# Early counting of places, an earlier gather, and the embedding product inside a first group of experts written apart

## The reference

```
x1 = LN1(alpha*x + W_out [pool_group(x) | mlstm_group(x)])
x2 = LN2(alpha*x1 + MoE(x1))            # top 4 of 32 experts, softmax router
y  = x2 + sigmoid(x2 @ W_pg) * (p @ W_ple)

logits = x1 @ w_router + b_router;  top_v, top_e = top_k(logits, 4);  gates = softmax(top_v)
for each expert e, for the tokens that chose it:
    h = xb @ w1[e] + b1[e]                                  # 1024 x 2048
    glu = min(h[:, ::2], 7);  lin = clip(h[:, 1::2], -7, 7)
    out = (glu * sigmoid(1.702*glu) * (lin + 1)) @ w2[e] + b2[e]   # 1024 x 1024
    MoE[token] += gate * out
```

## Time and profile before

| | us |
|---|---|
| three runs | 1112.04, 1112.07, 1110.48 |
| median | 1112.04 |
| span of the profiled execution | 1109.9 |
| TensorE busy | 1076.3 (97%) |
| VectorE busy | 436.3 (39%) |

### The profile page before, as it was taken

The page is one execution under the profiler, slowest core; times in us unless marked ns, Lnnn a source line. Parts: engine busy times, 40 slices in busy tenths (PEclk is TensorE's granted clock), DMA queues, the critical chain, the costliest instruction groups (busy, mean ns, idle before and its releaser), DMA issues.

```text
span 1109.9 us, 15169 instructions
## 1 busy us (share of the span) xinstructions
PE 1076.3 (97%) x5600; PEld 430.6 (39%) x5600; DVE 436.3 (39%) x1109; ACT 159.2 (14%) x306; POOL 82.2 (7%) x107
## 2 busy tenths in 40 slices
PE   8999999999999999999999999999999999999998
PEld 6787433333333333333333333333333333333334
DVE  1637773333333333333333333333333333323245
ACT  1532241000000000000000000000000000000033
POOL 0856511000000000000000000000000000000000
PEclk9999999999999999999999999999999999999999
DMA  9988989999999999999999999999999999999961
GB/s 315 267 340 332 311 343 390 428 427 428 429 428 430 428 428 430 427 429 429 427 429 429 426 430 429 428 429 429 428 427 429 427 426 429 427 425 429 428 271 40
DMA packets 52608, 440.63 MB, mean 397 GB/s; under 512 B 10544, under 2 KB 17964, under 8 KB 27381
## 3 DMA queue, kind: packets, MB, share of 16 engines
q1 hardware_dynamic: 52057, 439.53, 95.8%
q0 software_dynamic: 368, 0.57, 0.2%
q10 hardware_dynamic: 148, 0.07, 0.0%
HBM read 436.61 MB, written 3.77 MB: 397 GB/s over the span
## 4 chain that ended last, share of the span: by engine, by line
PE 64%; DMA 23%; DVE 9%; issue 2%; ACT 1%; POOL 1%; DVEq 0%; SPq 0%; POOLq 0%; ACTq 0%
PE bank L990 25%; DMA ring<-in_w_mlp 22%; PE bank L1061 16%; PE bank L590 6%; PE bank L949 4%; DVE proj L1619 3%; PE bank L769 3%; PE bank L1141 3%; DVE proj L1616 2%; DVE proj L1614 2%; PE bank L1042 1%; PE bank L962 1%; PE bank L984 1%; PE bank L1050 1%; DMA ring<-in_w_in 1%
## 5 line engine op out<-in xcount | busy, mean ns | idle before, releaser
L990 PE MATMUL bank<-ring,proj 128*64 128x512 f32 x2024 | 460.9, 597 | 13.1 <-DMA ring<-in_w_mlp 12.6
L1580 DVE SCALAR_TENSOR_TENSOR xT<-bank,proj,xT 128x512 f32<-128x512 f32 x128 | 90.2, 746 | 423.8 <-PE bank L949 422.5
L990 PEld LDWEIGHTS bank<-ring,proj 128*64 128x64 f32 x2024 | 140.8, 136 | 288.9 <-issue 260.5
L1061 PE MATMUL bank<-ring,pool_side 128*64 128x512 f32 x1024 | 226.8, 595 | 0.4 <-ACT pool_side L1951 0.4
L1061 PEld LDWEIGHTS bank<-ring,pool_side 128*64 128x64 f32 x1024 | 71.3, 137 | 133.5 <-issue 129.7
L1945 ACT ACTIVATE proj<-proj 128x256 f32<-128x256 f32 x64 | 26.7, 417 | 545.2 <-DVE proj L1613 544.2
L590 PE MATMUL bank<-xT,ring 128*128 128x264 f32 x320 | 77.1, 400 | 1.5 <-DMA ring<-in_w_in 1.5
L1571 DVE TENSOR_SCALAR proj<-bank,ln_rows_of_pairs 128x64 f32<-128x64 f32 x256 | 67.4, 335 | 24.5 <-PE bank L962 24.5
L949 PE MATMUL bank<-mixT 64*128 64x512 f32 x264 | 74.5, 641 | 0.9 <-ACT mixT L1954 0.5
L590 PEld LDWEIGHTS bank<-xT,ring 128*128 128x128 f32 x320 | 62.3, 197 | 14.3 <-issue 3.2
L928 PE MATMUL bank<-xreg,proj 128*64 128x512 f32 x248 | 58.7, 592 | 0.0
(11 more groups left out here) (369 smaller groups left out, 632.2 us busy)
## 6 DMA issues: line engine op xcount, KB each, us to landing
ring<-in_w_mlp SPq DMA_DIRECT2D x190, 2048.0 KB, 28.9
ring<-in_w_in SPq DMA_DIRECT2D x10, 1024.0 KB, 13.0
ring<-in_w_out SPq DMA_DIRECT2D x4, 1024.0 KB, 8.3
ring<-in_w_ple_gate SPq DMA_DIRECT2D x4, 1024.0 KB, 28.1
xreg<-in_x_prompt SPq DMA_DIRECT2D x4, 512.0 KB, 4.6
ring<-q_row SPq DMA_DIRECT2D x1, 2048.0 KB, 6.9
ring<-k_row SPq DMA_DIRECT2D x1, 2048.0 KB, 6.9
out<-ring SPq DMA_DIRECT2D x1, 2048.0 KB, 14.8
```

What stands on the lines that cost most here:

```text
L990: last = pe.matmul(bank[q][BLOCK * t:BLOCK * (t + 1), :], xgT[:, k % 4, k // 4, :], rows_[:, col:col + 512], start=False, stop=(k == KD - 1))
L1061: last = pe.matmul(bank[4][BLOCK * h:BLOCK * (h + 1), :], aT[:, m, BLOCK * t:BLOCK * (t + 1)], w[:, k % 2, 512 * h:512 * h + 512], start=F ...
L1580: ins = STT(total[:, c, s], ins_bank[h][:, :], gate_table[:, c, bass.ds(n, 1)], total[:, c, s], ALU.mult, ALU.add)
```

## The change

TensorE: the four early counts now stand ahead of `turn_quarter`, the sums of the early chunks between `turn_quarter` and `router(1, 6)`, and no embedding product stands in the handover. The first four experts are written apart from the loop, which starts at expert 4. In expert 0 a part of `early_embedding` follows each of the units 1 to 4, and `early_samples` follows the combination behind unit 5. The embedding of chunk 1 goes to banks 2 and 3 instead of 4 and 7, and before the gather for expert 1 TensorE waits until ScalarE has copied all three products. ScalarE's copies of the products move behind casts that it does for the sample rows. VectorE no longer waits for the products. SP loads `late[1]` behind pair n = 22 and no longer ahead of pair n = 16. `early_pT` moves to a space of its own, since `gates` is dead by then.

```
@@ banks @@
-        EMBED_BANKS = {0: (bank[1], bank[6]), 1: (bank[4], bank[7]), 2: (bank[5],)}
+        EMBED_BANKS = {0: (bank[1], bank[6]), 1: (bank[2], bank[3]), 2: (bank[5],)}
@@ SP @@
             load_next(14)
-            sp.wait_ge(sem("ple_ps"), 3)
-            load_late(1)
             for n in range(SLOTS, UNITS * STEP, 2):
                 sp.wait_ge(sem("units_used"), n - SLOTS + 2)
                 load_next(n)
+                if n == SLOTS + 6:
+                    sp.wait_ge(sem("ple_ps"), 3)
+                    load_late(1)
@@ TensorE, handover @@
-            turn_quarter(0)
-            turn_quarter(1)
-            router(1, 6)
...
                       start=False, stop=True).then_inc(sem("pos_ps"), 1)
+            turn_quarter(0)
+            turn_quarter(1)
             pe.matmul(bank[3][:, 0:3 * EXPERTS], ones16[0:1, :], far_row, start=True, stop=False)
             count_places(0, (1,))
             count_places(2, (1,))
+            router(1, 6)
             logit_rows(2)
-            pe.wait_ge(sem("ple_in"), 16)
-            early_samples()
...
             count_places(1, ()).then_inc(sem("pos_ps"), 1)
-            early_embedding(0, (0,))
@@ TensorE, expert(n, j, closing=0, opening=False) @@
+                    if opening and 1 <= k <= 4:
+                        early_embedding((k - 1) // 2, ((k - 1) % 2,))
...
                         combine(2, (j + 1) % 2)
+                        if opening:
+                            pe.wait_ge(sem("hotT_done"), 1)
+                            early_samples()
+
+                if opening:
+                    pe.wait_ge(sem("ple_done"), 3)
@@ TensorE, start of the experts @@
-            early_embedding(0, (1,))
-            early_embedding(1, (0, 1))
             pe.wait_ge(sem("places_split"), 1)
-            pe.wait_ge(sem("ple_done"), 1)
...
-            with pe.Fori(0, npass * EXPERTS - 2 * STEP, STEP) as n:
+            pe.wait_ge(sem("ple_in"), 16)
+            for j in range(STEP):
+                expert(j, j, opening=(j == 0))
+            with pe.Fori(STEP, npass * EXPERTS - 2 * STEP, STEP) as n:
@@ VectorE @@
-            dve.wait_ge(sem("ple_ps"), 3)
@@ ScalarE @@
-            act.wait_ge(sem("ple_ps"), 1)
-            act.copy(embedded_samples, EMBED_BANKS[2][0][:, 0:256]).then_inc(sem("ple_done"), 1)
...
-            embedded_early(0)
+            act.nop().then_inc(sem("out_done"), 1)
...
-            act.wait_ge(sem("ple_ps"), 3)
             act.copy(part_high, xtok[0:SAMPLES, 2, :]).then_inc(sem("part_cast"), 1)
+            embedded_early(0)
...
             act.copy(sample_parts[32:32 + SAMPLES, :], part_mid).then_inc(sem("sample_moved"), 1)
+            embedded_early(1)
...
             act.copy(sample_parts[0:SAMPLES, :], part_high).then_inc(sem("sample_moved"), 1)
+            act.wait_ge(sem("ple_ps"), 3)
+            act.copy(embedded_samples, EMBED_BANKS[2][0][:, 0:256]).then_inc(sem("ple_done"), 1)
```

12 lines of the change are left out of this document (5 added, 7 removed).

## The result

| | median, us | lowest to highest | executions |
|---|---|---|---|
| before | 1110.48 | 1108.33 to 1112.07 | 7 |
| changed | 1115.68 | 1112.07 to 1118.95 | 7 |

The ratio is 1.0043, with an interval from 1.0028 to 1.0058: the change makes the kernel 4.8 us slower by the ratio, 5.2 by the medians. The forecast was 2.0 us slower, 1114.0. The time lies in the range and the direction is the forecast one, but the size forecast was less than half of what came. That the time lies in the range is in part luck: the forecast built on 1112.04, the median of three runs, where seven have 1110.48, and this makes up for 1.6 us of the effect that it missed.

What follows compares the result with a forecast made beforehand. DMA engines bound the kernel: the fifth pair's limit moves from 181.7 to 183.2, +1.6 us, or +2.4 with small packets; taken as +2.0 on 1112.04, giving 1114.0 us. Own range 1113.2 to 1115.2; 8 in 10, 1110.4 to 1116.2.

Steps and rivals of the forecast that it cites:

- What bounds the kernel: Whole run: DMA engines set the end, at 428 GB/s, from the moment they are never idle again; TensorE's work doesn't.
- the tail doesn't change: End of the run: what follows the remaining bytes at 428 GB/s takes as long as before.
- The handover starts expert 0 earlier by 2.8 us: Handover ahead of expert 0: without the embedding products, its biases start at 150.85 against 153.64.
- the register load: Behind `spread_places`: loading the number of passes loses its cover and delays the biases by 0.8 us, bounds 0 and 1.3.
- `late[1]` in the full stream: Between fourth and fifth pair: the load, free before in an empty queue, now takes 2.45 us of DMA time.
- The sum of +2.0: Whole kernel: +1.6 us by the model, +2.4 with small packets of other queues, taken as +2.0.
- the later releases: Expert 0: its added products make the third, fourth and fifth pair releases 0.8, 1.8 and 1.6 us later.
- The rival with the slow clock: Handover: one 3.5 us stretch at the 1.2 GHz level costs 1.75 us, giving 1115.8; chance 0.12.
- No change: Rival, handover and expert 0: TensorE catches up partly, `late[1]` takes only dry time; +0.5 us, 1112.5; chance 0.17.
- the first release carries: Rival, first pair release: the queue resumes 2.8 us earlier and never runs dry afterwards, giving 1109.2; chance 0.13.
- No early start: Rival, handover: expert 0 starts less than 1 us earlier, the five products are paid in full, 1116; chance 0.03.

Runs made afterwards that it cites:

- the kernel that starved the queue for a moment in expert 7: Changed kernel with embedding products in expert 7, eight experts written apart, `late[1]` loaded behind the load group of experts 4 to 7: 1124.65 us, ratio 1.0137.
- load ahead: Changed kernel with TensorE's load of the number of passes moved ahead of the turning of the gathered rows: 1114.31 us, ratio 1.0032.
- the fillers: Four added products with unused results (256, 256, 384 and 512 columns) in the handover's waits of the changed kernel: 1112.75 us, ratio 1.0015.
- the thin products: Kernel before with its early embedding products 16 columns wide instead of 512 and 256, all in their old places: 1111.78 us, ratio 1.0007.

## Why the prediction was right in direction and wrong in size

**What bounds the kernel.** Right in the main. TensorE's waits for weights and its pace hardly move, and among kernels with the same loop the end follows the bytes left at 200: 2.4 MB more, 5.6 us. Between the two kinds of loop 0.6 to 2 us more come up behind 200, against the words that the tail doesn't change; and in the kernel that starved the queue for a moment in expert 7 a busy TensorE helped nothing.

**The handover starts expert 0 earlier by 2.8 us.** Right to 0.1 us (153.64 - 3.4 - 147.55 = 2.7), with its parts: the 0.8 us of the register load, and in expert 0 1.06 us for each embedding part where 1.0 was taken. The releases came 0.1 to 0.6 us after those of the sum, and expert 0's second product was 2.2 us late and not 1.6.

**`late[1]` in the full stream, 2.45 us.** Right in kind and somewhat too large: the load alone moved costs 2.0 us, the load taken out of the changed kernel gives back 0.5 to 1.9, most likely 1.4. It is the largest single part of the loss at an equal clock. Products and load don't simply add: with half of the products back in the waits the kernel is only 1.2 and 0.6 us above the kernel before (at 1.000 and 0.998), though this load is where the change put it.

**The sum of +2.0.** At an equal clock the change costs 2.6 to 2.7 us, within the forecast's own range of +1.2 to +3.2. What remains of the difference, 0.6 us, fits the later releases, and it also fits what comes up behind 200 in every kernel with the experts written apart (the last pair is under way 0.9 us longer); no run separates the two.

**The rival with the slow clock.** This is the step that was mis-sized, and what makes the measured loss more than twice the forecast one. It was named, but with a chance of 0.12, one stretch of 3.5 us and a price of 1.75 us. It was argued away with the stretch from 140.0 to 143.5, where TensorE was busy 2.43 of 3.50 us and the clock stayed full. But that stretch is followed, in the kernel before, by the samples, the gather and an embedding part, one behind the other from 144.30 to 149.5 without a gap; in the changed kernel the gather is followed by waits of 0.71, 0.21 and 0.80. The argument looked at the emptiest stretch by itself and not at what came behind it, which is just what the change takes away. And the fall doesn't last one stretch: in the long profiles the clock stays low for 13.7 us, until the products stand close again in expert 0, at a price of 4.8 us at the first release. It adds 1.7 us to the mean. The runs show that the products are the cause by taking them away from the kernel before (11 of 11 below 0.998, against 8 of 35 beside it) and by putting other products into the changed one (0 of 11, against 10 of 16). Half of them put back (6 of 12) doesn't settle anything. Taken together, the kernels without these products and without others in their place have 30 of 40 executions below 0.998 (changed 10 of 16, without the load 6 of 7, the two with the products in expert 7 3 of 4 and 5 of 5, load ahead 6 of 8), those with all of them in the handover 12 of 107. The moved load (1 of 11) and the moved counts (1 of 22) don't bring it. How the products act is less clear: a fall can begin at 141.0, ahead of the place where they stood, and the fillers, one of which runs at 140.3, filled waits on both sides of it. What is shown is that without dense products the clock stays low longer.

**No change, and the first release carries.** Both fell. The queue ran dry after the second and third release (172 and 166 GB/s), and the fifth was the limit. "No early start" fell with the biases at 147.55.

What stays open: why the fall comes in some executions of one program and not in others, and whether the embedding products keep it from starting or only from lasting; what of it the thin products' median hides; and what the experts written apart cost by themselves. No version here is clearly faster than the kernel before; the one with only the counts moved is its equal.

## What to carry to other kernels

Products that look as if they delay a chain of small dependent steps may be what keeps TensorE's clock from staying low through it: before moving them out, count which waits they fill, and put something in their place. Where a full DMA queue bounds the kernel, a load is free only in the gap in which the queue is empty, and every load that waits on SP holds up all loads behind it. And when two executions of a program differ, sort them by their mean granted clock before comparing medians; here this separates 2.65 us of the change from 1.7 us of the clock, and without it one experiment would have been read the wrong way round.

## What the runs showed of the hardware

The granted clock fell to the 1.2 GHz level in a handover in which TensorE never waited longer than about 0.8 us at once, and stayed there for 13.7 us with the engine busy 3.10, 2.69 and 2.76 of 3.40 us (already at the slower pace), and then, from 151.1 to 154.7, 3.60 of 3.60; from 154.7 on it was full again. The Trainium skill, TensorE: Matmul & The Clock Gate, section "A second HAM failure mode: psum-queue depth-cycling", says that frequent small pauses between groups of products, and not only long idle stretches, can make the clock swing. This case's traces agree in so far as the only waits in the handover are of 0.2 to 0.8 us, and the page's other case, long waits for a transfer, doesn't occur there; but the fall began at 141.0 behind the same work and waits as in a kernel whose clock stayed full, so that these waits alone bring it about isn't shown.

Whether it falls isn't fixed by the program: the same kernel has 1.000 in four executions and 0.992 to 0.994 in five, and is 6 us longer in these. A fall has no fixed length either: 3.4, 6.8, 13.7 and 17.1 us were seen.

One core moved 424 to 431 GB/s in every slice of the page over some 850 us, in all of these kernels but the starved one, as before the change; the 358 GB/s that the prediction weighed would have ended each of them far later.
